# A relative bias table in DRAM: one copy instead of 128, read back shifted with its keys reversed

## What is computed

```python
def band_geometry():
    i = jnp.arange(BLOCK)[:, None]
    j = jnp.arange(2 * BLOCK)[None, :]
    return i + BLOCK - j
...
    d = jnp.clip(band_geometry(), 0, WINDOW - 1)
    bias = rel_bias[t5_bucket(d)]
...
    logits = logits * (HEAD_DIM ** -0.5) + band_bias[None, None]
    logits = jnp.where(mask[None, :, None, None], logits, jnp.float32(-1e30))
```

## Time and profile before

| | |
|---|---|
| median of three runs | 2535.51 us |
| profiled execution, span from first to last instruction | 2534.7 us |
| TensorE busy in the span | 97% |
| mean granted TensorE clock | 0.982 of full speed |
| HBM read / written | 448.98 MB / 5.24 MB |

### The profile page before, as it was taken

One profiled execution on the slowest core, in us unless ns is written; L12 is line 12 of the kernel. 1 busy time (PEld: TensorE's weight loads), 2 busy tenths in 40 slices (PEclk: granted clock), 3 DMA queues, 4 the chain that ended last, 5 costly groups with the idle time before them and its releaser, 6 DMA issues.

```text
span 2534.7 us, 28733 instructions
## 1 busy us (share of the span) xinstructions
PE 2455.9 (97%) x11346; PEld 2020.0 (80%) x11346; DVE 1497.7 (59%) x2116; ACT 1106.5 (44%) x1388; POOL 0.2 (0%) x4
## 2 busy tenths in 40 slices
PE   8799999999999999999999999978999999999999
PEld 7688888878888888888878777757788888888887
DVE  4355799865544555577457576655655555554444
ACT  4344444544444444454355444424444444443333
POOL 0000000000000000000000000000000000000000
PEclk9899999999999999999899999989999999999999
DMA  7855566656665676665445343434566666666664
GB/s 228 226 159 183 169 191 187 198 192 208 192 197 169 206 259 193 187 224 181 137 158 172 115 142 116 161 104 126 154 190 189 191 190 190 186 190 190 202 204 142
DMA packets 126212, 456.12 MB, mean 180 GB/s; under 512 B 13643, under 2 KB 17900, under 8 KB 125052
## 3 DMA queue, kind: packets, MB, share of 16 engines
q1 hardware_dynamic: 126076, 454.27, 57.3%
HBM read 448.98 MB, written 5.24 MB: 179 GB/s over the span
## 4 chain that ended last, share of the span: by engine, by line
PE 92%; DVE 4%; DMA 2%; ACT 2%; issue 1%; SPq 0%; ACTq 0%; DVEq 0%
PE ps L409 85%; DMA t_raw<-w_in 1%; DVE t_wlo L367 1%; PE ps L298 1%; PE ps L539 1%; ACT t_whi L366 1%; PE ps L489 1%; PE ps L1344 1%; PE ps L384 1%; PE ps L522 0%; PE ps L453 0%; PE ps L925 0%; DVE t_st L426 0%; DVE t_A L284 0%; DMA t_raw<-w_kv 0%
## 5 line engine op out<-in xcount | busy, mean ns | idle before, releaser
L409 PE MATMUL ps<-t_whi,t_A 128*128 128x512 f32 (+2 forms) x5056 | 1578.0, 394 | 46.1 <-DVE t_wlo L367 26.6
L367 DVE TENSOR_TENSOR t_wlo<-t_raw,t_whi 128x1024 fp32r<-128x1024 f32 x805 | 981.1, 1223 | 937.6 <-ACT t_whi L366 933.9
L366 ACT ACTIVATE t_whi<-t_raw 128x1024 fp32r<-128x1024 f32 x805 | 848.2, 1058 | 1174.1 <-PE ps L409 1121.1
L409 PEld LDWEIGHTS ps<-t_whi,t_A 128*128 128x128 f32 x5056 | 950.2, 192 | 241.3 <-DVE t_wlo L367 28.5
L409 PE MATMUL ps<-t_wlo,t_A 128*128 128x512 f32 (+2 forms) x2528 | 988.7, 391 | 0.0
L409 PEld LDWEIGHTS ps<-t_wlo,t_A 128*128 128x128 f32 x2528 | 483.1, 191 | 99.8
L409 PE MATMUL ps<-t_whi,t_Y0a 128*128 128x512 f32 x1152 | 356.3, 391 | 0.0
L409 PEld LDWEIGHTS ps<-t_whi,t_Y0a 128*128 128x128 f32 x1152 | 215.6, 188 | 44.1
L409 PE MATMUL ps<-t_wlo,t_Y0a 128*128 128x512 f32 x576 | 224.4, 390 | 0.0
L409 PEld LDWEIGHTS ps<-t_wlo,t_Y0a 128*128 128x128 f32 x576 | 108.1, 188 | 22.7
L819 DVE SCALAR_TENSOR_TENSOR t_Y1a<-t_H,t_pp,t_Y1a 128x255 f32<-128x255 f32 (+29 forms) x240 | 96.2, 463 | 0.0
(11 more groups left out here) (286 smaller groups left out, 1107.0 us busy)
## 6 DMA issues: line engine op xcount, KB each, us to landing
t_raw<-w_in SPq DMA_DIRECT2D x376, 512.0 KB, 3.8
t_raw<-w_gu SPq DMA_DIRECT2D x176, 512.0 KB, 3.7
t_raw<-w_down SPq DMA_DIRECT2D x88, 512.0 KB, 4.1
t_raw<-w_branch SPq DMA_DIRECT2D x64, 512.0 KB, 3.8
t_raw<-w_out SPq DMA_DIRECT2D x64, 512.0 KB, 3.6
t_raw<-w_ck SPq DMA_DIRECT2D x16, 512.0 KB, 3.6
t_raw<-w_cv SPq DMA_DIRECT2D x16, 512.0 KB, 4.2
t_raw<-w_cq SPq DMA_DIRECT2D x8, 512.0 KB, 3.5
```

Source lines behind the costliest of these rows:

```text
L366: a = S.do(lambda e: e.activation(whi[:, s, 0:n], raw[:, d % NR, 0:n], ACT.Copy), tok, free, cost=1.0)
L367: b = V.do(lambda e: e.tensor_tensor(wlo[:, s, 0:n], raw[:, d % NR, 0:n], whi[:, s, 0:n].bitcast(F32), ALU.subtract), a, free, cost=1.15)
L409: fn = lambda e, x=x, w=w, kt=kt, k=k, t=t, j=j, bk=bk: e.matmul(bk[:, 0:n], x[:, u["k0"] + kt, t * P:(t + 1) * P], w[:, k, :], start=(kt ...
```

## The change

The table is written once per head (24 KB). The one-hot matrix is reversed along its 384 columns, so that a row of the table runs the other way. The read goes in four transfers of four heads and 512 KB each, one after each of four successive chunks, and starts two chunks after the write, not five; partition p starts one element further than partition p-1, in the same 384 values. `B1` then holds the keys in reverse order, and VectorE reads it with a step of -1.

```diff
-        w = load(dr["toep"], gt[0:16, :].unsqueeze(1).to_broadcast([16, P, 384]), c)
+        w = load(dr["toep"], gt[0:16, :], c)
         last_use["table"] = w
-        yield 5
-        src = bass.AP(dr["toep"].tensor, 127, [[383, P], [384 * P, 16], [1, 256]])
-        last_use["B1"] = load(B1[:], src, w)
+        yield 2
+        quarters = []
+        for h in range(0, 16, 4):
+            src = bass.AP(dr["toep"].tensor, 1 + 384 * h, [[1, P], [384, 4], [1, 256]])
+            quarters.append(load(B1[:, h:h + 4, :], src, w))
+            yield
+        last_use["B1"] = quarters
         flags["B1"] = True
...
-                                                             in1=B1[:, heads, 256 - nk:256], op0=ALU.mult,
+                                                             in1=B1[:, heads, nk - 1::-1], op0=ALU.mult,
                                                              op1=ALU.add)]
...
-            oh[b, m] = 1
+            oh[b, 383 - m] = 1
         else:
-            oh[32, m] = 1
+            oh[32, 383 - m] = 1
...
-    dr["toep"] = nc.dram_tensor("toep", [16, P, 384], F32).ap()
+    dr["toep"] = nc.dram_tensor("toep", [16, 384], F32).ap()
```

## The result

| | before | after |
|---|---|---|
| median, lowest, highest (4 runs each) | 2535.49, 2531.09, 2536.18 us | 2518.15, 2515.06, 2518.83 us |
| ratio after / before | | 0.9932, 95% interval 0.9919 to 0.9945 |
| span of the profiled execution | 2534.7 us | 2513.8 us |

The changed kernel is 17.3 us faster; 2518 us was forecast, with 17.4 us for the stop. The range was 2513 to 2525.

A forecast was written before the change was run, and what follows sets the result against it. TensorE, in order and 97% busy, was taken as the bound, stopped by a weight load queued behind the table write. Median 2535.5 less 17.4 us for the stop, other terms nothing, gave 2518; range 2513 to 2525.

The forecast's parts named there:

- the stop: TensorE idle from 70 to 85 us for a late weight load, then restarting at half clock: 17.39 us lost.
- The bound: Whole span: in-order TensorE, busy 97%, sets the time; a microsecond it stands still is lost unless made up later.
- R1 to R5: Five weight loads behind the table write on SP's list; claimed to stand in line behind its 3 MB until 81.0 us.
- The write and SP's wait: Table write on SP's list: 24 KB lands within 4.4 us, so SP's wait at the first read costs nothing.
- q0: First of the four table reads on SP's list; waits for the write, reached about 1.5 us after that has landed.
- The reads: Four table reads among the weight loads: 1.5 us per quarter taken, so TensorE does not stop.
- R6: Weight load behind all four reads, the tightest: claimed to land at 67.7 us, 15.8 early.
- two readings: Old write's slowness: few ports reached by partitions 0 to 15, or rows read again being slow, 0.6 us longer.
- The backward read: VectorE's twelve bias additions of 0.684 us with step -1: no change taken; rival of double cost, 6.4 us, chance 0.04.
- The flag: B1's flag goes up after six chunks, not five: no TensorE instruction changes place, cost nothing.
- The slower rival: Around 75 to 90 us, reads choke on one small piece of DRAM; 2581 us at the far end; chance 0.10.
- 4Q - 21.8: TensorE's stop in us, where positive, at the weight load behind all four reads; Q is the time of one quarter read.

The follow-up runs named there:

- partitions 8 apart: Changed kernel plus an extra 3 MB write to a tensor nobody reads, taken from 16 partitions, 0, 8, 16 to 120: 2520.33 us, ratio 0.9946.
- The kernel with the same row: Changed kernel with one 2 MB read for the four, all 2048 rows being the same 1 KB of DRAM: 2534.86 us, ratio 0.9995.

## Why the prediction was right

*The bound.* Right. One in-order engine, one stop, and a load behind a slow transfer at its end. The chain of waits named the load, but only SP's timeline named what stood in front of it. One sentence of it is too simple: "It was not SP that was stopped." SP waited for no token ahead of R1 to R5, but issuing these five held it for some 27 us. Nothing in the sum hangs on it.

*The size of the loss.* Right: 17.39 us read off the matmuls, 17.5 from the write to the first addition in two profiles. The 17.3 between the medians agree to a tenth by luck: the interval of the ratio allows 14 to 20.5 us. Idle time alone would have given 15.6; the 1.75 at half clock belong to the stop. The first bias addition starts at 89.9, where 91.3 was worked out; most of the 1.4 is the early half-clock stretch that the profile before happened to have.

*The write and SP's wait.* Right: 3.4 us against 4.4 taken, and no wait at q0. What a long wait there would have cost by itself no run shows: where it lasted to 80.67, TensorE stood still for R1 anyway.

*The reads.* Right: 1.5 us per quarter taken, 1.4 per transfer in the line of reads and loads. R6 landed at 67.5, where 67.7 was worked out. That is closer than the working deserves: the profile after runs some 1.3 us ahead, and R6 came 12.7 us behind R2 (54.8), not 11.2. One detail of "what would show it" missed: the reads were to land within 4 us of their issue and took 6.1, as they share the line with the weight loads. Under some 15 us of cover it costs nothing.

*Why the write was slow.* The prediction left two readings. The partitions 8 apart speak for the first: the source partitions set the rate (17.9 us against 34.5), with the tile read as the one thing not held equal. With the other reading the sum would have been the same within a microsecond.

*The backward read.* Right: 684 ns both ways. *The flag.* Right: TensorE, VectorE and ScalarE have the same instructions in the same order; only SP's list differs.

*The slower rival.* Its mechanism was real, its price was not. Even with all rows in 1 KB a quarter takes 7.2 us, short of the 9.4 from which the change would have lost; by the prediction's sum, 4Q - 21.8, that is a stop of 7 us. The kernel with the same row came out level with the one before, since its one read puts all 2 MB ahead of R3, which is due earlier than R6. As the table is laid out, with 6 KB per quarter, the case is not met. A chance of 0.10 for slower was given for want of any row; a read of one small piece by all partitions, tried by itself, would have bounded Q and so all but excluded it.

## What to carry to other kernels

A transfer that no engine waits for can still be the one that stops the kernel: look at what is in line ahead of the late load, and compare its GB/s with that of the same bytes elsewhere (here 101 against some 350). Replicating rows on the way out of a few neighbouring partitions is the slow way to make copies; write once and let a shifted read make them, as long as the readers do not all share too small a piece (6 KB was fast here, 1.5 KB slow). The cover of a buffered stream can be worked out from the trace as a deadline for each load, and then every delay has a price: nothing up to the deadline, one for one after it, plus the restart at half clock behind the long stops (8.3 us and more here).

## What the runs showed of the hardware that I had not expected

A read of 2 MB from DRAM into 128 partitions took 10.2 to 10.9 us when its rows lay in 24 KB, and 30.7 to 31.9 us when they lay in 1.5 or 1 KB. With one and the same row the DMA engines were not even busy. Stretches of that run (the columns of the earlier trace rows; the last three are granted clock, busy share of the DMA engines, and GB/s):

```profile
60.00:65.00 5.00, 5.00 (x23) 4.13 (x22) 2.02 (x2) 2.14 (x3) 0.00 (x0) 1.00 0.23 79
65.00:70.00 5.00, 5.00 (x23) 4.13 (x22) 1.23 (x1) 0.00 (x0) 0.00 (x0) 1.00 0.25 74
70.00:75.00 5.00, 4.70 (x21) 3.57 (x19) 0.00 (x0) 0.00 (x0) 0.00 (x0) 1.00 0.38 81
```

About 80 GB/s at a busy share of 0.2 to 0.4, where the old write had 101 at 0.9: a slow transfer need not show as busy engines. With all rows in 1.5 KB the traffic was as slow, but the busy share was 0.60 to 0.97:

```profile
60.00:65.00 5.00, 5.00 (x23) 4.13 (x22) 2.01 (x3) 2.12 (x2) 0.00 (x0) 1.00 0.60 73
70.00:75.00 5.00, 4.24 (x19) 3.19 (x17) 0.00 (x0) 0.00 (x0) 0.00 (x0) 1.00 0.97 75
```

Whether the two have the same cause is not shown.
